# The causal mask of the row-maximum scores: a VectorE addition in PSUM in place of a TensorE product with the identity

## What is computed

```
def _masked_probs(s, mask):
    s = jnp.where(mask, s, NEG)
    m = jnp.max(s, axis=-1, keepdims=True)
    p = jnp.where(mask, jnp.exp(s - m), 0.0)
    return p / jnp.maximum(jnp.sum(p, axis=-1, keepdims=True), TINY)
...
    s = jnp.einsum('btgrd,bkgd->bgrtk', qg, kw).astype(jnp.float32) * SCALE
    dlt = q_pos[:, None] - k_pos[None, :]
    mask = (dlt >= 0) & (dlt < WINDOW) & (k_pos >= 0)[None, :]
    p = _masked_probs(s, mask)
    return jnp.einsum('bgrtk,bkgd->btgrd', p, vw)
```

## Time and profile before

| | |
|---|---|
| median of 3 runs | 1184.65 us (1184.32 to 1190.48) |
| the profiled execution | 1184.23 us |
| its span, first to last instruction | 1182.5 us |
| TensorE clock granted, mean | 0.986 of full speed |
| PE / PEld busy | 1129.5 us (96%) / 1039.7 us (88%) |
| DVE / ACT / POOL busy | 441.1 us (37%) / 372.6 us (32%) / 465.9 us (39%) |

### The profile page before, as it was taken

How to read it: one execution, slowest core, us unless ns; L and a number is a source line. 1 busy time by engine, 2 the same in 40 slices (tenths; PEclk the granted TensorE clock), 3 DMA queues, 4 the chain that set the end, 5 groups by cost and what they waited for, 6 DMA issues and landing times.

```text
span 1182.5 us, 20739 instructions
## 1 busy us (share of the span) xinstructions
PE 1129.5 (96%) x8502; PEld 1039.7 (88%) x8502; DVE 441.1 (37%) x620; ACT 372.6 (32%) x497; POOL 465.9 (39%) x265
## 2 busy tenths in 40 slices
PE   6999999999999999898999899999999999999995
PEld 5999998999999988665555499999999999999994
DVE  4857650011212231548653534453332332301015
ACT  5224242233112144344545223333322322212211
POOL 5342536465434333116411134343443435344440
PEclk9999999999999999999999989999999999999997
DMA  7426212333632315431216662323223232222201
GB/s 250 128 72 212 85 59 72 108 90 99 204 89 72 106 42 164 162 100 37 55 38 224 221 227 72 108 74 106 90 88 106 72 106 71 98 80 90 98 27 72
DMA packets 109363, 126.28 MB, mean 107 GB/s; under 512 B 10671, under 2 KB 102983, under 8 KB 107776
## 3 DMA queue, kind: packets, MB, share of 16 engines
q1 hardware_dynamic: 105784, 120.19, 32.3%
q10 hardware_dynamic: 3527, 5.39, 1.4%
HBM read 111.38 MB, written 16.17 MB: 108 GB/s over the span
## 4 chain that ended last, share of the span: by engine, by line
PE 77%; issue 12%; POOL 5%; DVE 3%; ACT 1%; DMA 1%; SPq 0%; POOLq 0%; ACTq 0%; DVEq 0%
PE D L1812 57%; PE E L1812 6%; PE D L2063 5%; POOL w_lo L732 4%; PE D L2048 1%; PE D L2049 1%; DVE nmax L1526 1%; PE E L2029 1%; PE E L2119 1%; PE E L1998 1%; PE E L2024 1%; DMA slot<-in_cache_win 0%; ACT pT L1017 0%; PE E L2079 0%; DVE yT L1133 0%
## 5 line engine op out<-in xcount | busy, mean ns | idle before, releaser
L732 POOL TENSOR_TENSOR w_lo<-w_raw,w_hi 128x1024 fp32r<-128x1024 f32 x164 | 401.5, 2470 | 552.8 <-ACT w_hi L824 532.4
L824 ACT ACTIVATE w_hi<-w_raw 128x1024 fp32r<-128x1024 f32 x164 | 164.2, 1050 | 289.1 <-PE D L1812 241.1
L1812 PE MATMUL D<-hH,w_hi 128*128 128x260 f32 x1152 | 238.3, 288 | 1.4 <-DVE exl L1210 1.4
L1812 PE MATMUL D<-hH,w_lo 128*128 128x260 f32 x1152 | 232.5, 283 | 0.0
L1812 PE MATMUL D<-hL,w_hi 128*128 128x260 f32 x1152 | 232.3, 283 | 0.0
L1812 PEld LDWEIGHTS D<-hH,w_hi 128*128 128x128 f32 x1152 | 178.7, 189 | 6.0 <-issue 3.8
L1812 PEld LDWEIGHTS D<-hH,w_lo 128*128 128x128 f32 x1152 | 178.2, 189 | 0.0
L1812 PEld LDWEIGHTS D<-hL,w_hi 128*128 128x128 f32 x1152 | 177.9, 189 | 0.0
L1812 PE MATMUL D<-onH,w_lo 128*128 128x260 f32 x816 | 164.5, 283 | 0.0
L1812 PE MATMUL D<-onH,w_hi 128*128 128x260 f32 x816 | 164.3, 282 | 0.0
L1812 PE MATMUL D<-onL,w_hi 128*128 128x260 f32 x816 | 164.2, 283 | 0.0
(11 more groups left out here) (359 smaller groups left out, 1466.0 us busy)
## 6 DMA issues: line engine op xcount, KB each, us to landing
w_raw<-in_w_in SPq DMA_DIRECT2D x64, 512.0 KB, 5.0
w_raw<-in_w_ffn_in SPq DMA_DIRECT2D x44, 512.0 KB, 4.4
slot<-in_cache_kv SPq DMA_DIRECT2D x64, 128.0 KB, 2.7
w_raw<-in_w_ffn_out SPq DMA_DIRECT2D x16, 512.0 KB, 3.9
rows_b<-rnorm_d SPq DMA_DIRECT2D x8, 512.0 KB, 4.8
w_raw<-in_w_nsa_out SPq DMA_DIRECT2D x8, 512.0 KB, 8.8
slot<-in_cache_win SPq DMA_DIRECT2D x16, 256.0 KB, 4.6
w_raw<-in_w_o SPq DMA_DIRECT2D x8, 512.0 KB, 4.3
```

What stands on the lines that cost most here:

```text
L732: nc.gpsimd.tensor_tensor(wl[b][:, x], raw[b][:, x], wh[b][:, x].bitcast(F32), ALU.subtract)\
L824: nc.scalar.activation(wh[b][:, x], raw[b][:, x], ACT.Copy).then_inc(hi_done, 1)
L1812: ins = mm(out2[:, a, 0:HALF], lhsT, rhs[:, a * HALF:(a + 1) * HALF], start=first, stop=last)
```

## The change

Each product with the identity is taken out of `row_scores`, and the product of queries and keys is now a group of its own (`stop=True`). In `row_max` DVE first adds the table to the diagonal block of both branches, in place in PSUM, in one instruction of 128 x 2 x 128 elements; it waits until that is done (`settle`, a wait on DVE's own semaphore) and then reduces as before.

```
--- before.py
+++ after.py
@@ -1520,6 +1520,10 @@
                 nk, e = (qi + 1) * P, 2 * (n % 2)
                 src = E[:, e, 0:2 * nk].rearrange("p (b k) -> p b k", b=2) if qi < 2 else E[:, e:e + 2, 0:nk]
                 dve.wait_ge(max_mm, n + 1)
+                own = src[:, :, qi * P:nk]
+                step(nc.vector.tensor_tensor(own, own, causal_r[:, :].bitcast(F32).unsqueeze(1).to_broadcast([P, 2, P]),
+                                             ALU.add))
+                settle()
                 a = qi // 2
                 if g >= 2:
                     dve.wait_ge(nmax_turned, 2 * (g - 2) + a + 1)
@@ -2021,14 +2025,10 @@
                 q = qst[b][:, qi, h, :]
                 if qi < 2:
                     out = E[:, e, 0:2 * nk].rearrange("p (b k) -> p b k", b=2)
-                    mm(out, q, k1[b][:, :, 0:nk], start=True, stop=False)
-                    ins = mm(out[:, :, qi * P:nk], ident_r[:, :],
-                             causal_r[:, :].unsqueeze(1).to_broadcast([P, 2, P]), start=False, stop=True)
+                    ins = mm(out, q, k1[b][:, :, 0:nk], start=True, stop=True)
                 else:
                     for br in range(2):
-                        mm(E[:, e + br, 0:nk], q, k1[b][:, br, 0:nk], start=True, stop=False)
-                    for br in range(2):
-                        ins = mm(E[:, e + br, qi * P:nk], ident_r[:, :], causal_r[:, :], start=False, stop=True)
+                        ins = mm(E[:, e + br, 0:nk], q, k1[b][:, br, 0:nk], start=True, stop=True)
                 ins.then_inc(max_mm, 1)
```

## The result

The changed kernel is slower, as forecast. Its median is 1193.52 us (20 executions, 1188.34 to 1198.02) against 1184.05 for the kernel before (20, 1180.38 to 1190.48): a ratio of 1.0081, 95% interval 1.0070 to 1.0092. The forecast was 1191.8 us, within 1186 to 1198. The profiled execution of the changed kernel (its record, as this text calls the trace of one execution) took 1190.47 us, with a span of 1188.7.

The account below looks back on a forecast made before the run. It took DVE, with little slack in windows 2 and 3, to set windows 1 to 3 once the additions land there: -0.5 + 0.8 + 4.0 + 3.3 = +7.6 us on 1184.23 gives 1191.8, range 1186 to 1198.

Parts of the forecast that it names:

- both bounds, 0.33 and 0.48: Limits for one DVE addition: 0.33 us from a pair of reductions, 0.48 from an in-place operation in E; totals 1187 and 1195.
- PE gets its time back: Rival: PE's 2.9 us per window remain in windows 0 and 1 (-5.8 us, 1178.4), or in all four (1172.7); chance 0.06.
- The sum of +7.6 us: All four windows together, -0.5 + 0.8 + 4.0 + 3.3 us, on the profiled execution's 1184.23: 1191.8 us.
- The gap of 0.03 us and the lost overlap of 0.09: In each row maximum, the reduction starts 0.03 us behind the addition and loses a 0.09 us early start.
- The rival that took them for nothing: Rival: the wait behind each addition costs nothing, saving 0.12 us per row maximum; +2.8 us, 1187.0; chance 0.24.
- Windows 1 to 3: DVE's row maxima, transposes, other work and holes set the lengths: 22.0, 27.1 and 25.3 us, or +0.8, +4.0 and +3.3.
- The terms of window 0: Start, row maxima up to the thirteenth, then PE and POOL steps put POOL's clearing at 487.2 or 487.3: -0.5 us.
- PE's 2.9 us come to nothing there: Window 1: the product time taken off PE gains nothing, since PE, where ahead, waits for a place in E.
- The holes of rows four and five: Window 1: these rows' maxima start 1.55 us apart without the product against 1.06 of DVE work; 0.5 us each.
- the fall of PE's clock: Rival: after 2.5 us waits in windows 2 and 3 PE falls to 1.2 GHz, 1.6 us each; 1195.0; chance 0.16.
- it decides between 1.74 and 2.76: Clock rival's threshold: a PE wait of 1.74 us left the clock at 1.00, one of 2.76 was followed by 0.59.
- No line beyond 610 us costs more or less: Sign expected in the new profile: lines after 610 us cost the same as before.

Follow-up runs that it names:

- the kernel with the sum aside: Kernel before, products kept, plus an addition that in windows 1 to 3 writes to an unread SBUF buffer, so the reduction does not wait: 1188.72 us, 1.0059.
- the runs with the change in two windows: Against the kernel before, the change in windows 0 and 1 alone: 1183.80 us, 1.0015; in windows 2 and 3 alone: 1192.02 us, 1.0091.
- with the products kept: Kernel before, identity products kept, with the in-place addition and its wait put in as well: 1194.72 us, 1.0099.
- the later transpose: PE's second transpose two steps later, its transfers one step later: changed kernel 1186.93 us (1.0033), kernel before 1182.04 (0.9991), no mask 1172.83 (0.9926).
- the second record of before: The kernel before run again unchanged for another trace: 1182.84 us.
- the first experiments: Follow-up runs against the kernel before, beginning with the changed kernel without the addition (0.9929) and the kernel before with the addition put in (1.0099).
- the one record at 0.983 above: Second trace of the unchanged changed kernel, mean clock 0.983, with half clock behind window 3 and near 182, 491 and 685 us; that run's median 1190.54 us.
- the second comparison: The changed kernel run again against the kernel before: 1190.54 against 1183.60 us, 1.0057 (1.0039 to 1.0075).

## Why the prediction was right, and what it missed

**The addition: right.** 0.43 us was forecast from the one operation of that size, 424 ns was measured in 64 of them. The neighbour of the same size and form was the right row; both bounds, 0.33 and 0.48, were off by more.

**The product's cost: a misreading, and luck that the sum did not need it.** The forecast charged each of the 96 products with the 0.12 us of one with 256 columns, 11.5 us in all and 2.9 per window. 64 of them have 128 columns and cost 0.17 us in pairs, so that the row gives 9.3 and 2.3, and the rival "PE gets its time back" would have been worth 4.6 or 9.3 us, not 5.8 or 11.5. The sum of +7.6 us stayed clear of it, because it took PE's relief as nothing in windows 1 to 3 and built window 0 from DVE's row maxima.

**The wait: right.** The gap of 0.03 us and the lost overlap of 0.09, read from operations of other sizes, came out as 0.12 when the dependence was taken away. The rival that took them for nothing is refuted. The Trainium skill, "VectorE: DVE Perf Modes", section "The DRAIN you can't avoid", measured on a chain of copies that a semaphore after each costs nothing extra; that does not carry over to this pair. The same section says that a next operation that is not held starts earlier, and the kernel with the sum aside agrees (0.34 us against 0.46).

**Windows 0 to 3: right, to 0.25 us.** Window 0 was forecast at -0.5. From the first operation of DVE to POOL's clearing it was 487.78 - 470.15 = 17.63 us and is 485.62 - 468.45 = 17.17, and that first operation comes 0.12 earlier behind its row score (idle 0.64, not 0.76): -0.58. Windows 1 to 3 were forecast at +0.8, +4.0 and +3.3 and came at +0.83, +3.74 and +3.32. The terms of window 0 as the forecast lists them add up to 487.1, not 487.2 or 487.3, which would be -0.7. That the loss lies in windows 2 and 3 and hardly in window 1 was the core of the argument, and the runs with the change in two windows show it; that DVE's other work makes the difference is what the busy times say.

**PE's relief: small, as forecast, but not nothing in window 1.** The forecast said PE's 2.9 us come to nothing there. Without the relief window 1 is another 1.15 us longer. The holes of rows four and five (counted from zero), which the forecast counted as PE's, stand in the changed kernel at 0.43 and 0.40 us, and with the products kept they are only 0.2 longer together. Most of the 1.15 lies in holes that the changed kernel hardly has, ahead of the third, ninth, thirteenth and fourteenth row maximum, some 0.8 us: there a row score with its products ends after DVE is ready for it, which the forecast did not look at.

**The clock: a rival that half came true.** The forecast set the fall of PE's clock beside its own case, with a chance of 0.16, as happening behind both windows or neither. It happened behind window 3 in each of the five records with a wait of 2.06 to 2.28 us there, and in none of the eight with 1.79 or less; from the end of the last copy of window 3 to the memset these five took 6.8 us and five of the eight, without the later transpose, 5.2, whatever the wait: it cost 1.6 to 1.7 us, the price that the rival gave it. Behind window 2, in the same five records, equal waits were followed by a full clock. So what failed in the rival is "if it falls after both", and with it "it decides between 1.74 and 2.76": waits of 2.36 to 2.67 us left the clock at 1.00 in three records, and the very wait of 2.76 on which the upper end rested was followed by half clock in five records of 13. The length of a wait does not decide by itself. What does is not known from these runs, nor why window 3's place lost its clock every time. The Trainium skill, "TensorE: Matmul & The Clock Gate", part 1, has the clock fall to half behind idle stretches of PE; window 3 agrees, and the places of full clock after equal waits show that the length of one wait does not tell it here.

**"No line beyond 610 us costs more or less": not quite.** From the memset to the end of the span the three records of the changed kernel took 575.4, 575.8 and 575.5 us, the two of before 576.5 and 577.1. 0.7 to 1.7 us come back there. The place is just behind the prompt's attention, at full clock: from the memset to PE's first product with the sample tokens' new keys (L2192) the two records of before take 51.07 and 51.71 us and the three of the changed kernel 50.08 to 50.29. A transpose of the sample keys waits there in before, here the second record, for DVE's copy of the ones before it, and that copy stands in DVE's order behind a normalizer that waits for a transfer:

```profile
650.24 0.17 DVE L1539 TENSOR_SCALAR sums<-sums 128x16 f32<-128x16 f32 x1 [1.59 <-DMA sums<-obuf]
...
652.79 0.63 PE L2175 MATMUL E<-ident,slot 128*128 128x128 f32 x4 [1.28 <-DVE kTs L1621]
```

In the first record these waits are 0.63 and 0.93 us; in the changed kernel PE has none there and the normalizer waits 0.22 us at most. Why the transfer comes in time there isn't settled; the kernel before with the later transpose has no such wait of PE either. This and the 1.6 us behind window 3 nearly cancel, so the sum of +7.6 us fits the records better than its parts deserve: from the second record of before to the third of the changed kernel it is 1190.31 - 1182.84 = +7.5.

**The two comparisons.** +9.5 us in the first, +6.9 in the second, where 9 to 10 had been expected. In the second the changed kernel's mean clock was 0.986 or 0.987 in seven of nine executions; in the first it was 0.984 or less in 17 of 20, while the 23 executions of before that ran beside the first experiments had a median of 0.987. Executions of the changed kernel at 0.986 or 0.987 took 1188.3 to 1191.1 us in both. So the further 2.5 us of the first comparison go with a lower clock in those executions. In which stretch those executions lost it was not recorded, but for the one record at 0.983 above; it stays open. So does what the chip has to do with it: the second comparison was made on another chip than the experiments.

**A faster kernel.** Without any mask in the row maxima, and with the later transpose, the kernel takes 1172.83 us, 0.9926 (0.9906 to 0.9945) of before: faster than both. The maximum is then taken over later keys too and cancels in the quotient. It is safe only as long as no later key's score tops a row's own maximum by so much that its exponentials vanish; other inputs weren't tried.

## What to carry to other kernels

Work moved from the busiest engine to a less busy one costs what it takes in the stretch where it lands: DVE was busy for 37% of the span, yet windows 2 and 3 grew by the part of the additions that found no idle time of DVE there, and PE's relief was worth little. Price a removed instruction by its own shape: a product of 128 columns cost 0.085 us, not the 0.12 of one with 256. Here an in-place addition ahead of a dependent reduction cost 0.12 us beyond the 0.34 that it takes without the dependence. Before moving a term ask whether the result needs it at all. Look for a wait whose place in the order is free: two steps later for one transpose took 2.3 to 2.5 us off the stretch in kernels with no addition, though their runs' times cannot tell that from nothing, and 6.2 with it.

## What the runs showed that was not expected

- Equal waits of PE did not bring equal clocks. A wait of 2.06 to 2.28 us left the clock at 1.00 behind window 2 and was followed by 0.51 to 0.60 over 3.4 us behind window 3, in each of five records. PE's busy time ahead of both is alike (19.87 us of 26.85 and 19.52 of 25.35). A wait of 2.67 us left it at 1.00, and one of 2.76 was followed by half clock in five of 13 records.
- Stretches at half clock near 182, 491 and 680 us come and go between executions of one kernel (0.57 and 0.72 in the same 12 us), and the time goes with the mean clock: in the first comparison the changed kernel took 1188.3 to 1190.5 us at 0.986 and 0.987, and 1194.6 to 1198.0 at 0.978 and 0.979. A stretch chosen between them repeated to 0.1 us.
- The addition takes the same time in place in PSUM (424 ns) and from PSUM into SBUF (419 ns).
